# ScalarE rounds the weight panels that a group of matmuls released one group later (first network)

## The reference, cut to what matters

```python
u = rms_norm(x, g_mix) * (1 + sc_a) + sh_a            # scales and shifts come from cond @ w_ada
proj = u @ w_in                                       # fox q k v, latents, stick-breaking q k v, 3 x 1024 gates
y_fox, y_mla, y_sb = three attentions, 8 heads each   # softmax, softmax, stick-breaking
merged = sum(sigmoid(gate_b) * (y_b @ w_o_b))         # over the three branches
x = x + gt_a * (merged @ w_out)
u = rms_norm(x, g_ffn) * (1 + sc_f) + sh_f
x = x + gt_f * ((silu(u @ w_gate) * (u @ w_up)) @ w_down)
```

## Time and profile before

| | us |
|---|---|
| median of 3 runs | 2476.86 (2463.89 to 2481.15) |
| the profiled execution | 2472.51 |
| its span, from the first to the last instruction | 2470.7 |
| mean granted TensorE clock in it | 0.949 of full |
| first layer of the first network: first projection to its last `down` group | 70.5 to 616.5 in the span |
| second layer: the same | 630.4 to 1172.1 |

### The profile page before, as it was taken

How to read it: one execution, slowest core, us unless ns; L and a number is a source line. 1 busy time by engine, 2 the same in 40 slices (tenths; PEclk the granted TensorE clock), 3 DMA queues, 4 the chain that set the end, 5 groups by cost and what they waited for, 6 DMA issues and landing times.

```text
span 2470.7 us, 36391 instructions
## 1 busy us (share of the span) xinstructions
PE 2227.5 (90%) x13724; PEld 1945.1 (79%) x13724; DVE 1634.2 (66%) x2617; ACT 1174.1 (48%) x2021; POOL 32.4 (1%) x18
## 2 busy tenths in 40 slices
PE   1899988999899998999786989989998899898998
PEld 0897778999897788999575566768775788888998
DVE  5557766984458776984477588938584723575983
ACT  3345563563445564563434634435253324644772
POOL 4000000000000000000000000000000000000000
PEclk8899998999899998999898999989999899998999
DMA  6456633865456633865352063535351323313553
GB/s 257 137 179 235 211 101 120 263 231 180 136 178 235 210 111 120 268 226 182 117 178 104 3 202 128 179 106 183 121 179 60 128 94 111 103 52 128 187 179 113
DMA packets 107181, 385.08 MB, mean 156 GB/s; under 512 B 11664, under 2 KB 16272, under 8 KB 105744
## 3 DMA queue, kind: packets, MB, share of 16 engines
q1 hardware_dynamic: 75680, 272.66, 32.8%
q10 hardware_dynamic: 31344, 110.24, 12.8%
HBM read 381.81 MB, written 1.05 MB: 155 GB/s over the span
## 4 chain that ended last, share of the span: by engine, by line
PE 70%; DVE 15%; DMA 6%; ACT 5%; issue 3%; ACTq 1%; DVEq 0%; SPq 0%
PE ps L863 18%; PE ps L867 18%; PE ps L866 18%; DVE ada_junk L1776 6%; DMA ring<-tape_in 3%; DMA work<-adas_in 3%; PE ps L880 3%; PE ps L884 3%; PE ps L883 3%; DVE ring_l L1751 2%; PE ps L1064 1%; PE ps L1199 1%; DVE part L1751 1%; ACT ring_r L1240 1%; PE ps L1149 1%
## 5 line engine op out<-in xcount | busy, mean ns | idle before, releaser
L863 PE MATMUL ps<-part,ring_l 128*128 128x256 f32 (+1 forms) x3808 | 1188.1, 312 | 100.2 <-DVE part L1861 39.1
L867 PE MATMUL ps<-part,ring_r 128*128 128x256 f32 (+1 forms) x3808 | 1171.5, 308 | 0.0
L866 PE MATMUL ps<-part,ring_r 128*128 128x256 f32 (+1 forms) x3808 | 1170.6, 307 | 0.0
L863 PEld LDWEIGHTS ps<-part,ring_l 128*128 128x128 f32 x3808 | 731.5, 192 | 163.1 <-issue 73.7
L1240 ACT ACTIVATE ring_r<-ring 128x1024 fp32r<-128x1024 f32 x511 | 535.4, 1057 | 633.3 <-DMA ring<-tape_in 520.3
L1751 DVE TENSOR_TENSOR ring_l<-ring,ring_r 128x1024 fp32r<-128x1024 f32 x511 | 616.0, 1220 | 221.8 <-ACT ring_r L1240 219.4
L866 PEld LDWEIGHTS ps<-part,ring_r 128*128 128x128 f32 x3808 | 733.8, 193 | 31.6
L867 PEld LDWEIGHTS ps<-part,ring_r 128*128 128x128 f32 x3808 | 731.7, 192 | 33.1
L1776 DVE SCALAR_TENSOR_TENSOR ada_junk<-work 128x1024 bf16<-128x1024 f32 x272 | 345.6, 1270 | 45.6 <-DMA work<-adas_in 30.1
L880 PE MATMUL ps<-ring_l,part 128*128 128x512 f32 x264 | 106.1, 402 | 11.0 <-ACT work L1588 6.2
L883 PE MATMUL ps<-ring_r,part 128*128 128x512 f32 x264 | 105.9, 401 | 0.0
(11 more groups left out here) (198 smaller groups left out, 1798.0 us busy)
## 6 DMA issues: line engine op xcount, KB each, us to landing
ring<-tape_in SPq DMA_DIRECT2D x518, 512.0 KB, 3.4
work<-adas_in ACTq DMA_DIRECT2D x176, 512.0 KB, 4.3
work<-ada_first_in ACTq DMA_DIRECT2D x8, 1024.0 KB, 16.2
work<-bias_in ACTq DMA_DIRECT2D x1, 2048.0 KB, 9.8
work<-cond_in ACTq DMA_DIRECT2D x1, 1536.0 KB, 8.0
x<-x_t_in ACTq DMA_DIRECT2D x1, 1024.0 KB, 12.8
x<-ctx_in ACTq DMA_DIRECT2D x1, 1024.0 KB, 5.6
x<-dist_in ACTq DMA_DIRECT2D x1, 1024.0 KB, 7.4
```

Of the source, the lines that this page charges most:

```text
L863: mm = pe.matmul(dst, lhsT=wl, rhs=mr, start=(k == 0), stop=False)
L866: pe.matmul(dst, lhsT=wr, rhs=mr, start=False, stop=False)
L867: mm = pe.matmul(dst, lhsT=wr, rhs=ml, start=False, stop=(k == len(moving) - 1))
```

## The change

`finished(name)` no longer rounds the panels that group `name` released, but those that the last group with panels before it released. The first such call in a layer rounds nothing. `read_last` is set back at the layer's end, where the call that rounds all the rest stays. Nothing is changed for VectorE, TensorE, SyncE or the second network.

```diff
@@ -1229,6 +1229,12 @@
         def _(act):
             base = [0]
             made = [RING]
+            read_last = [0]
+
+            def round_behind(read):
+
+                round_panels(read_last[0] + RING)
+                read_last[0] = read
 
             def round_panels(n):
 
@@ -1274,7 +1280,7 @@
 
                     act.wait_ge(*done(name, l))
                     if name in READ:
-                        round_panels(READ[name] + RING)
+                        round_behind(READ[name])
 
 
                 def shifted(n, shift):
@@ -1442,6 +1448,7 @@
                     finished(f"down{f}")
                 round_panels(PANELS_1 + RING)
                 made[0] = RING
+                read_last[0] = 0
 
 
             base[0] = DEPTH * PANELS_1
```

## The result

| | us |
|---|---|
| median before | 2474.82 (2463.89 to 2481.15, 4 runs) |
| median after | 2435.41 (2432.68 to 2440.32, 4 runs) |
| ratio | 0.985 (95%: 0.9816 to 0.9884) |
| the profiled execution after | 2440.32 (before 2472.51) |
| its span | 2438.2 (before 2470.7) |

The change takes 39 us off the time, 29 to 46 by the interval of the ratio. It is far from the 2456 that was forecast: the gain is nearly twice as large. The pair of profiled executions shows only 32.5 us of it, because the one after is the slowest of its four.

A forecast was written before the change was run, and what follows sets the result against it. TensorE, busy 90% of the span, bounds the kernel. Waits 20.6 plus clock 5.0, less 1.4 in `down` and 3.4 at layer ends, made 20.8 us less: 2456 from the median, range 2437 to 2475.

The forecast's parts named there:

- TensorE's some 35 us of waits: Both layers' waits for the copy 13.5, rests 11.4, stick-breaking probabilities 7.0, last square 3.1 us: nearly all there is to win.
- the copy: Attention steps, copy of a head's probabilities (L1384): 8.3 of TensorE's 13.5 us of waits go; 5.2 stay.
- the rests: Branches and `w_out` groups, TensorE's waits for rests (L1751): 6.2 of 11.4 us go.
- the last square: Behind `w_out7`, ScalarE's wait ahead of a rounding and the squares: all 3.1 us of TensorE's waits go.
- the end of attention: Last attention step, TensorE's wait for stick-breaking probabilities (L2011), 3.5 us per layer: 1.5 per layer goes, 3.0 us in all.
- the copy's waits before 255 us: Attention stretch whose roundings had no landing wait: VectorE is as slow as TensorE; with its second-layer twin 5.2 us stays.
- the formula of the Trainium skill: DMA time as fixed 2.0 us plus bytes over 436e3 per us: 3.2 us for 512 KB, so no landing outlasts a step.
- a third of 15.3 us: Slow-clock stretches behind TensorE's longer waits, three losing 3.4 us and three 1.7 us: 5 us of 15.3 won back.
- The rival in which the clock comes back as well: Waits below 1 us leave the clock alone: the other 10 us and some kept waits won, 25 to 40 us less; 20%.
- waits for a subtraction: In `down`, ends of the third and seventh group: too few tiles ready, 0.35 us each, 1.4 us in two layers.
- the first layer's end: Behind `down7`, six roundings instead of three before the squares take 6.0 us: 1.7 us later, 3.4 us for both ends.
- `down` doesn't starve: Rival: TensorE waits 2.3 us at each of 14 `down` group ends, 32 us; 15 us more in all, 2492; 8%.

The follow-up runs named there:

- the two halves: The kernel before with one group late only in attention, branches and w_out: 2434.29 us, ratio 0.9855; only in projections and feed-forward: 2472.65 us, 1.001.
- the late order everywhere else: The kernel before with one group late only in projections and feed-forward, at once in attention, branches and w_out: 2472.65 us, ratio 1.001.
- the end of the step: Gate's panel rounded at its own attention step's end: against the kernel before 2454.88 us (0.9955); with branches and w_out one group late too, 2441.6 us (0.9912).

## Why the prediction was right, and where it was off

**Where the time is: right.** The argument that of 322.2 us of landing waits only those ahead of TensorE's some 35 us of waits count is what the two halves showed: 115 us of landing waits taken away outside these places moved nothing, and all of the gain lies inside them.

**The waits: right in sum.** Predicted 20.6 us, gone are 22.7: for the copy 10.4 (predicted 8.3), the rests 5.5 (6.2), the last square 3.1 (3.1), the end of attention 1.3 for L2011 and 2.4 for VectorE's probabilities (3.0 at L998 before, 0.6 at L993 after), whose row was not in my sum (3.0 predicted for the two together). One detail was wrong: the copy's waits before 255 us, which I took to be VectorE's and to stay, fell from 3.9 to 1.3 us. Another looks wrong and is right. In the `w_out` groups I expected ScalarE's wait for a landing to shrink to some 0.6 us, and its rows still say 1.4 us per group. Here are ScalarE's and VectorE's timelines after the change, behind the last `w_out`:

```profile
396.67 1.06 ACT L1246 ACTIVATE ring_r<-ring 128x1024 fp32r<-128x1024 f32 x1 [1.47 <-DMA ring<-tape_in]
...
399.46 1.06 ACT L1246 ACTIVATE ring_r<-ring 128x1024 fp32r<-128x1024 f32 x1 [1.42 <-DMA ring<-tape_in]
400.42 0.40 ACT L1427 ACTIVATE x<-x 128x256 f32<-128x256 f32 x1
```

```profile
399.26 0.48 DVE L2029 SCALAR_TENSOR_TENSOR x<-ps,mod,x 128x256 f32<-128x256 f32 x1 [0.28 <-PE ps L867]
```

VectorE is released by the group's end at 399.26. ScalarE waits for the same end and then for the landing, until 399.46, and the row puts its whole idle time down to the later of the two. The landing itself held it for 0.2 us. Before, the same 1.42 us stood behind a group that had long ended, at 415.69. So the square starts 1.4 us behind the group's end now (399.06 on TensorE), where it started 4.2 us behind it, at 419.89, and TensorE's sum goes through without a wait. Part of the 140.4 us that are left of ScalarE's landing waits may be such waits for a group's end.

One reading of mine was wrong without harm to the sum. The landing of 9.0 us, of which I said that it would leave 2.7 us behind a step of attention, is that of a load at the very start of the kernel, 1.2 us into the span, and it is there with small modulation loads too. In the first network from 60 us on the longest is 7.4 us. And the formula of the Trainium skill that I set beside it (DMA: Bandwidth & Descriptors, the section on the anatomy of one DMA) is given there for DMAs that GpSimd issues; SyncE issues these loads. That its 3.2 us comes near the measured 3.4 is no test of it.

**The clock: the term that was off in size.** I took a third of 15.3 us, 5 us, "in attention VectorE is close behind and would eat most of it". TensorE's busy time in the first network fell by 11.2 us in one trace of the change and by 13.5 in the other, more than twice what I took. That is against the one trace of the kernel before; the mean of it and of the late order everywhere else, which takes the same time, is 1046.9, and the mean of the two traces of the change 1037.5, which makes 9.4 us of clock and 20.5 of idle time. With this term at 11.2 my sum would be 27 us, 2450 by the median. The rival in which the clock comes back as well (25 to 40 us, 2444) is thus the nearest, and I gave it 20%. Its condition, that waits below 1 us leave the clock alone, held at `w_out` (0.62 and 0.52 us, full clock), and the stretch that was offered for it, full clock where waits are short, was the better evidence. That the result (2439.7 us by the ratio) lies inside my range is owed to the range's width: it reached down to that rival's case.

**The costs: a little too high.** Four waits for a subtraction, as counted, 0.25 us each against 0.35. One of them:

```profile
562.21 0.39 PE L863 MATMUL ps<-part,ring_l 128*128 128x256 f32 x1 [0.26 <-DVE ring_l L1758]
```

At the first layer's end six roundings of 5.79 us together, as forecast (6.0), and 1.5 us more of waiting (predicted 1.7). At the second layer's end I predicted the same; the wait went from 8.14 to 7.80 us instead. In kernels whose order there is as before it is 7.0 to 8.3 us, so the change costs less there than this scatter, and the 1.7 us don't show. Costs of 2.2 us, then, where I had 4.8. `down` doesn't starve: these four waits come to 1.0 us.

**What I don't have.** The profiled pair gives 32.5 us, the medians 39 and, on the other chip, 32 (2470.65 to 2438.95); the sum of measured terms, 19.9 of idle time and 11.2 of clock, explains the first and the last. I don't have a term for the 7 us between, and the chips and executions scatter by more (the kernel before by 17 to 23 us on one chip; the second network's stretch, with the same code in all kernels, by 10 us between traces). Nor did a run set the clock apart from the waits: that short waits keep it is read from traces of kernels which differ in both. And why 1.32 us at 218 us cost no clock before, and 1.33 us with 0.65 ahead of it did after, is a reading of three stretches (the second trace of the change being the third) and no test.

## What to carry to other kernels

In an order written by hand, a wait for something that may be late belongs where nothing stands behind it that another engine will need soon; asking at the same place for an earlier item does that without moving anything, while moving the wait elsewhere puts it ahead of another customer (the end of the step, 12 to 14 us worse). Price such a change by the waits of the bounding engine and not by those of the waiting one (115 us of these were worth nothing), and count the clock behind such waits as a term of its own, here some 9 us (5 to 14) beside 20 us of waits. Where a queue of preparations and a short piece of work with a waiting customer come together, as at a layer's end, the short piece goes first: 8 us for a few lines.

## What the runs showed that I had not expected

- The clock reacted to less than I had thought. Behind 1.64 us with 0.52 shortly after it, fourteen matmuls took 3.14 instead of 1.8 us; behind 0.65 and 1.33 us the clock from 215 to 235 us was 0.74; behind 1.32 us alone it stayed 1.00, in the kernel before and in the second trace of the change.
- A side stream of loads costs a kernel whose order leaves it no room: cutting the modulation loads took 14 us off the kernel before and more than halved the copy's waits, but nothing clear of the scatter off the changed one.
- The clock's share differs between traces of unchanged code: TensorE's busy time in the second network, the same 6096 matmuls each time, was 1161.2 to 1171.0 us.
- A row's idle time names only what came last. Where an instruction waits for two things, the first can be nearly all of it, as with the 1.42 us of which 0.2 were the landing's.
- VectorE, 99 times waiting for a rounding in the first network instead of 52 and for 165.7 instead of 67.6 us, was never late for it by more than 0.3 us as TensorE sees it.
